# One product for each step of the merge's coefficient chain, and other gates for the pool rows' loads

## The chip, the cores and the metric

The kernel runs on one core of a Trainium2 chip. The metric is the device time of a whole execution in microseconds (us). TensorE (PE) multiplies, VectorE (DVE), ScalarE (ACT) and GpSimd (POOL) work elementwise, and SyncE (SP) issues nearly all DMA transfers. PE reads and writes nothing in DRAM: it takes operands from SBUF and leaves results in the eight banks of PSUM.

## What is computed

One encoder layer on two sequences (`x_prompt`, `x_sample`), each 1024 tokens of 1024 channels, in fp32. Cut to what matters here:

```
h = rmsnorm(x, norm_mix);  z = h @ w_in
a = pool_mixer(z[..., :512], pool_maps, pool_scale) @ w_up_pool
b = attention_branch(z[..., 512:]) @ w_up_attn
gates = sigmoid(h @ w_gate + b_gate)
x = x + (g_a * a + g_b * b) @ w_out
h = rmsnorm(x, norm_ffn)
x = x + (silu(h @ w_ffn_gate) * (h @ w_ffn_up)) @ w_ffn_down
y = rmsnorm(x, norm_final)

# end of attention_branch, three groups of four heads:
alpha  = softmax(stack(lses), axis=0)        # weights of the 3 groups
merged = sum(alpha[..., None] * outs, axis=0)
```

## The kernel before

The two sequences (s = 0, 1) follow one another. Every fp32 product is made of three single-pass matmuls: an operand is split into a rounded part (`_hi`) and the rest (`_lo`), and the small-by-small term is left out (`three`, L1207 to L1209). The projections use Strassen's scheme: a pair of weight tiles `n` takes seven **products**, numbered m = 7n + o, each of 4 x 3 = 12 matmuls of 128x512. The front of a sequence is products 0 to 132 (19 pairs); then come the up products (pool and attention rows by their up weights), `w_out`, the FFN.

The order on each engine is written out by hand: each engine has its own loop over m, and code hung on `if m == ...` stands at that place of that engine's queue. ACT makes `t_hi` (`operand_hi`, L1703) three products ahead, POOL the `t_lo` (`low_part`, L988) behind it, and PE waits for `t_ready`. After the first product of a pair ACT copies its bank out (`first_product`, `u`, L1715), and PE's third product of that pair, which adds to the same bank, waits for this copy. DVE makes the Strassen sums from PSUM (`after_product`: L2222, L2225, L2228, L2230, L2232); the last product of a pair adds to the bank that L2228 reads, and so waits for L2228.

Around m = 117 to 132 the **merge** of the three attention groups runs beside products of the pairs 16 to 18. Its **coefficient chain**: SP loads the softmax statistics (`st_all`, L697), DVE forms differences (`merge_differences`, L2325 to L2328), ACT takes the exponential (`merge_weights`, L1800), DVE normalizes (`merge_coefficients`, L2336 to L2341), ACT rounds (`round_coefficients`, L1805), DVE takes the rest (`split_coefficients`, L2348), PE turns the 24 coefficient columns (L1370) and ACT copies them out (`evict_coefficients`, L1814). Then twelve **spreads** (L1384) follow, two behind each of six products from SPREAD0 on; each writes a coefficient's row to all its channels in a bank. DVE multiplies (`merge_step`, L2368, counted by `ct_read`); POOL adds two of three groups (`merge_sum`, L1008, `two_merged`) and DVE the third (`merge_last`, L2378, `merged` after each half). There are four such pairs of sums. `MERGE0` is 118 and `SPREAD0` is 123.

The **pool rows** of the mixer (four tiles `ml` of 128x1024, 512 KB each) were written to DRAM before and are loaded (`load_mixed`, L724) into the SBUF space that the attended rows `oT` leave. ACT and DVE split them (`mix_hi` L1826, `mix_lo` L2391). The first up product needs `mix_lo` of row tile k at its matmul 3k+1, and `wu_lo`, the split up weights, which POOL makes (L1113) after `merged` and after ACT's `wu_hi` (L1835). Weights `wu_raw` are loaded at L733 and L734 (256 KB and 128 KB for each of two buffers), the gates `gl` at L743 (1 MB).

Of the kernel before, what the change touches and what calls it, by code (L numbers as in the profile page):

```python
# [84 lines left out]
VT_AFTER = {7 * (N_QK + g) + (4, 6, 7, 8)[c]: (g, c) for g in range(GROUPS) for c in range(4)}  # L85
MERGE0 = ATT0 + N_UNITS + 4


SPREAD0 = MERGE0 + 5

SUM_AFTER = {SPREAD0 + 4 + (3 * i + 1) // 2: (i // 2, i % 2) for i in range(4)}
MERGE = [(q, h, g) for q in range(2) for h in range(2) for g in range(GROUPS)]
# [167 lines left out]
def due(name, s, n):  # L260

    step = 16 if name in DMA_SEMS else 1
    return (s * PER_SEQ[name] + n) * step
# [50 lines left out]
def encoder(nc, x, w_in, maps, w_up_pool, w_up_attn, w_gate, w_out, w_fg, w_fu, w_fd,  # L314
# [3 lines left out]
    with ctx:  # L318
# [206 lines left out]
        def _(sp):  # L525
# [193 lines left out]

            def load_mixed(s, gs, batches):  # L720

                sp.wait_ge(merged, due("merged", s, batches))
                for g in gs:
                    sp.dma_start(ml[g][:, :], mix_rows[g]).then_inc(ml_in[g], 16)  # L724

# [78 lines left out]
            for s in range(SEQS):  # L804
# [6 lines left out]
                for m in range(FRONT):  # L811
# [53 lines left out]
                    if m == SPREAD0 + 3:  # L865
                        sp.wait_ge(mix_stored, due("mix_stored", s, 8))
                        load_mixed(s, range(3), 1)
                    if m == SPREAD0 + 6:
                        sp.wait_ge(ct_full, due("ct_full", s, 12))
                        load_up(s, 0)  # L870
                        load_up(s, 1)
                        load_mixed(s, range(3, 4), 2)
                    if m == FRONT - 4:
# [730 lines left out]
        def _(act):  # L1604
# [301 lines left out]
            for s in range(SEQS):  # L1906
# [34 lines left out]
                for m in range(FRONT):  # L1941
# [23 lines left out]
                    if s and m in (3, 4):  # L1965
                        final_stats(s - 1, 3 + m)
                    if m == MERGE0 - 1:
                        merge_weights(s)
                    if m == MERGE0:
                        round_coefficients(s)  # L1970
                    if m == SPREAD0 - 1:
                        evict_coefficients(s)
                    if m == SPREAD0 + 8:
                        up_hi(s, 0)
                        up_hi(s, 1)
# [100 lines left out]
        def _(dve):  # L2076
# [415 lines left out]
            for s in range(SEQS):  # L2492
# [24 lines left out]
                for m in range(FRONT + 1):  # L2517
# [23 lines left out]
                    elif stage == 1:  # L2541
                        window_sums(s, e, (2, 3))
                        window_means(s, e)
                    if m == MERGE0 - 1:
                        make_selector(s)
                        merge_differences(s)
                    if m == MERGE0:
                        merge_coefficients(s)
                        split_coefficients(s)
                    f = 2 * (m - SPREAD0 - 1)  # L2550
# [150 lines left out]
```

## Time and profile before

| | us |
|---|---|
| median of 3 runs | 2529.12 |
| lowest and highest | 2526.83, 2532.96 |
| the profiled execution: time | 2531.72 |
| its span, first to last instruction | 2529.8 |
| mean granted TensorE clock | 0.997 |

The profile is one execution. The span is what its rows cover; the time has another 1.9 us around it. A timeline row gives start, duration, engine, line, operation, output from inputs, count, and in brackets the engine's idle time ahead of it with what ended it. A matmul of 128x512 has a duration of 0.39 us but the next begins 0.23 us after it, so idle time in brackets is 0.16 us less than the delay of a start.

### The profile page before, as it was taken

Reading aid. Unit: us, or ns where it says so; the run is one execution under the profiler, and the core shown is the slowest. Engines: PE = TensorE matmul, PEld = TensorE weight load, DVE = VectorE, ACT = ScalarE, POOL = GpSimd, SP = SyncE. Lnnn points to the kernel's source line nnn. Section 1 sums busy time; section 2 is a strip of 40 time slices with the busy share of each in tenths; the row PEclk is TensorE's granted clock in tenths of the full one; section 3 lists DMA queues with packets and bytes.
Section 4 is the critical chain, followed back from the end, with each engine's and each line's share of the span. In section 5 each row is a group of like instructions: output and inputs, shape, how many; then the busy total and the mean of one; then the engine's idle time right before and its main releaser. Section 6 shows DMA issues by size and latency. Waiting matters only on the chain.

```text
span 2529.8 us, 32980 instructions
## 1 busy us (share of the span) xinstructions
PE 2495.5 (99%) x11900; PEld 2055.7 (81%) x11900; DVE 1283.3 (51%) x1784; ACT 1035.6 (41%) x2000; POOL 1712.4 (68%) x1269
## 2 busy tenths in 40 slices
PE   7999999999999999999999999999999999999998
PEld 6788878788888888888888887878888888888887
DVE  7852545653522222378988444556453222223768
ACT  5224554444533333345452345534453233233445
POOL 6666446644888888765787654574468888887544
PEclk9999999999999999999999999999999999999999
DMA  4444455472233333375453535555522333335544
GB/s 149 153 137 140 153 164 169 150 258 93 87 95 118 100 92 122 104 237 176 145 164 100 162 101 168 168 168 187 217 92 80 121 96 96 117 96 174 184 129 142
DMA packets 329024, 354.40 MB, mean 140 GB/s; under 512 B 30368, under 2 KB 236064, under 8 KB 327328
## 3 DMA queue, kind: packets, MB, share of 16 engines
q1 hardware_dynamic: 327424, 349.04, 43.7%
q10 hardware_dynamic: 1440, 3.25, 0.3%
q8 instruction: 97, 1.59, 0.3%
q14 instruction: 63, 0.52, 0.1%
HBM read 250.85 MB, written 101.38 MB: 139 GB/s over the span
## 4 chain that ended last, share of the span: by engine, by line
PE 91%; DVE 3%; ACT 1%; DMA 1%; issue 1%; POOL 1%; SPq 0%; ACTq 0%; DVEq 0%
PE ps L1207 28%; PE ps L1209 28%; PE ps L1208 28%; PE ps L1322 2%; PE ps L1283 2%; PE ps L1300 1%; DMA st_rows<-st 1%; PE ps L1340 0%; PE ps L1228 0%; ACT S L1672 0%; PE ps L1361 0%; DVE mix_lo L2391 0%; DVE X L2088 0%; PE ps L1255 0%; ACT squares L1617 0%
## 5 line engine op out<-in xcount | busy, mean ns | idle before, releaser
L1207 PE MATMUL ps<-S,t_hi 128*128 128x512 f32 (+1 forms) x2328 | 916.4, 394 | 10.7 <-ACT u L1715 4.1
L1209 PE MATMUL ps<-S,t_lo 128*128 128x512 f32 (+1 forms) x2328 | 904.4, 389 | 0.0
L1208 PE MATMUL ps<-S,t_hi 128*128 128x512 f32 (+1 forms) x2328 | 903.7, 388 | 0.0
L1207 PEld LDWEIGHTS ps<-S,t_hi 128*128 128x128 f32 x2328 | 438.7, 188 | 106.5 <-issue 12.6
L1209 PEld LDWEIGHTS ps<-S,t_lo 128*128 128x128 f32 x2328 | 438.9, 189 | 90.4
L1208 PEld LDWEIGHTS ps<-S,t_hi 128*128 128x128 f32 x2328 | 439.0, 189 | 86.2 <-issue 1.0
L988 POOL TENSOR_TENSOR t_lo<-wraw,t_hi 128x512 fp32r<-128x512 f32 x185 | 248.2, 1342 | 216.3 <-ACT t_hi L1703 213.0
L988 POOL TENSOR_TENSOR t_lo<-wraw_ff,t_hi 128x512 fp32r<-128x512 f32 x225 | 293.0, 1303 | 74.4 <-ACT t_hi L1703 70.3
L988 POOL TENSOR_TENSOR t_lo<-R,t_hi 128x512 fp32r<-128x512 f32 x154 | 221.2, 1442 | 175.4 <-ACT t_hi L1703 175.3
L1703 ACT CAST t_hi<-wraw_ff 128x512 fp32r<-128x512 f32 x225 | 139.9, 623 | 368.9 <-PE ps L1209 368.4
L1207 PE MATMUL ps<-t_hi,d_hi 128*128 128x512 f32 x616 | 240.9, 391 | 0.6 <-POOL t_lo L988 0.6
L1209 PE MATMUL ps<-t_hi,d_lo 128*128 128x512 f32 x616 | 239.9, 389 | 0.0
L1208 PE MATMUL ps<-t_lo,d_hi 128*128 128x512 f32 x616 | 239.8, 389 | 0.0
L1703 ACT CAST t_hi<-wraw 128x512 fp32r<-128x512 f32 x185 | 115.6, 626 | 244.2 <-PE ps L1209 238.0
L2443 DVE TENSOR_TENSOR d_lo<-d_raw,d_hi 128x512 fp32r<-128x512 f32 x154 | 146.4, 954 | 94.5 <-ACT d_hi L1891 93.6
L2222 DVE TENSOR_TENSOR u<-u,ps 128x512 f32<-128x512 f32 x82 | 56.2, 685 | 265.7 <-PE ps L1209 265.3
L1891 ACT CAST d_hi<-d_raw 128x512 fp32r<-128x512 f32 x154 | 95.5, 620 | 172.8 <-PE ps L1209 151.1
L2225 DVE TENSOR_TENSOR v<-u,ps 128x512 f32<-128x512 f32 x82 | 56.3, 686 | 207.4 <-PE ps L1209 207.2
L988 POOL TENSOR_TENSOR t_lo<-t,t_hi 128x512 fp32r<-128x512 f32 x74 | 97.7, 1321 | 93.6 <-ACT t_hi L1703 93.5
L988 POOL TENSOR_TENSOR t_lo<-t_ff,t_hi 128x512 fp32r<-128x512 f32 x90 | 117.6, 1307 | 31.5 <-ACT t_hi L1703 31.4
L1207 PEld LDWEIGHTS ps<-t_hi,d_hi 128*128 128x128 f32 x616 | 115.6, 188 | 25.3 <-POOL t_lo L988 1.2
L1122 POOL TENSOR_TENSOR wo_lo<-wo_raw,wo_hi 128x1024 fp32r<-128x1024 f32 x32 | 82.3, 2582 | 79.3 <-ACT wo_hi L1857 79.3
(182 smaller groups left out, 3903.3 us busy)
## 6 DMA issues: line engine op xcount, KB each, us to landing
d_raw<-d_rows SPq DMA_DIRECT2D x154, 256.0 KB, 2.8
d_rows<-act_f SPq DMA_DIRECT2D x110, 256.0 KB, 2.1
wraw_ff<-w_ffn_up SPq DMA_DIRECT2D x44, 512.0 KB, 4.6
R<-w_ffn_down SPq DMA_DIRECT2D x88, 256.0 KB, 3.1
wraw<-w_in SPq DMA_DIRECT2D x42, 512.0 KB, 5.8
sp_rows<-gst SPq DMA_DIRECT2D x80, 256.0 KB, 2.4
wraw_ff<-w_ffn_gate SPq DMA_DIRECT2D x40, 512.0 KB, 5.0
wo_raw<-w_out SPq DMA_DIRECT2D x36, 512.0 KB, 4.0
```

Source lines behind the costliest of these rows:

```text
L988: nc.gpsimd.tensor_tensor(shape(t_lo[r][:, :]), src, shape(t_hi[r][:, :]).bitcast(F32), ALU.subtract).then_inc(t_ready, 1)
L1122: nc.gpsimd.tensor_tensor(wo_lo[r][:, :], wo_raw[op % 3][:, :], wo_hi[r][:, :].bitcast(F32), ALU.subtract).then_inc(wo_ready, 1)
L1207: nc.tensor.matmul(o_ps, w[0], r[0], start=begins, stop=False, skip_group_check=True)
L1208: nc.tensor.matmul(o_ps, w[0], r[1], start=False, stop=False, skip_group_check=True)
L1209: return nc.tensor.matmul(o_ps, w[1], r[0], start=False, stop=ends, skip_group_check=True)
L1283: ins = nc.tensor.matmul(ps[:, first + h, c:c + wid], qk[p % 2][rows, 0, b * P:(b + 1) * P], qk[p % 2][rows, 1, lo:lo + wid], start=True, ...
L1322: ins = nc.tensor.matmul(ps[rows, 5, c0 + us.start * P:c0 + us.stop * P], V[p % 2][0:length, v, rows], pT[0:length, us, h * len(tiles) + c ...
L1703: nc.scalar.copy(dst, src).then_inc(thi_ready, 1)
L1891: nc.scalar.copy(d_hi[d % 4][:, :], d_raw[d % 4][:, :]).then_inc(dhi_ready, 1)
L2222: V_.tensor_tensor(u, u, b1, ALU.add).then_inc(sums_done, 1)
L2225: V_.tensor_tensor(v1[:, :], u, b2, ALU.add).then_inc(sums_done, 1)
L2443: V_.tensor_tensor(d_lo[d % 4][:, :], d_raw[d % 4][:, :], d_hi[d % 4][:, :].bitcast(F32), ALU.subtract).then_inc(d_ready, 1)
```

## The change

The chain gets later and separate places: `merge_differences` and `merge_weights` stand at m = 119 (from 117), `merge_coefficients` at 120 (from 118), `round_coefficients` and `split_coefficients` at 121 (from 118), `evict_coefficients` at 123 (from 122). PE's turn of the coefficients is behind product 122 instead of 121, and the spreads stand behind products 124 to 129 instead of 123 to 128; so do DVE's steps that read them and POOL's clearing and sums, each one product later, except POOL's fourth sum, which stays behind the low part of 132. ACT's `up_hi` stays at 131. The loads of the pool rows get gates of their own: tile 0 four steps, tile 1 POOL's second sum, tile 2 the first merged half, tile 3 ten steps (all were `merged`, one half for tiles 0 to 2 and two for tile 3). The load of the up weights moves from SP's place 129 to 130, while the first gates' load stays at 129.

```diff
-SPREAD0 = MERGE0 + 5
-SUM_AFTER = {SPREAD0 + 4 + (3 * i + 1) // 2: (i // 2, i % 2) for i in range(4)}
+WEIGHTS0 = MERGE0 + 1
+SPREAD0 = MERGE0 + 6
+SUM_AFTER = {min(SPREAD0 + 4 + (3 * i + 1) // 2, FRONT - 1): (i // 2, i % 2) for i in range(4)}
...
-            def load_mixed(s, gs, batches):
-                sp.wait_ge(merged, due("merged", s, batches))
+            def load_mixed(s, gs):
                 for g in gs:
+                    if g in (0, 3):
+                        sp.wait_ge(ct_read, due("ct_read", s, 4 if g == 0 else 10))
+                    elif g == 1:
+                        sp.wait_ge(two_merged, due("two_merged", s, 2))
+                    else:
+                        sp.wait_ge(merged, due("merged", s, 1))
                     sp.dma_start(ml[g][:, :], mix_rows[g]).then_inc(ml_in[g], 16)
...
-                    if m == MERGE0 - 1:
+                    if m == WEIGHTS0:
                         merge_weights(s)
-                    if m == MERGE0:
+                    if m == WEIGHTS0 + 2:
                         round_coefficients(s)
                     if m == SPREAD0 - 1:
                         evict_coefficients(s)
-                    if m == SPREAD0 + 8:
+                    if m == FRONT - 2:
                         up_hi(s, 0)
                         up_hi(s, 1)
...
-                    if m == MERGE0 - 1:
+                    if m == WEIGHTS0 - 2:
                         make_selector(s)
+                    if m == WEIGHTS0:
                         merge_differences(s)
-                    if m == MERGE0:
+                    if m == WEIGHTS0 + 1:
                         merge_coefficients(s)
+                    if m == WEIGHTS0 + 2:
                         split_coefficients(s)
```

On ACT, at the coefficient chain of the first sequence (`u` is the bank copy, `d` the differences), there stood:

```order
L1800 ACTIVATE d_303<-d_303 128x96 [waits diff_ready]
L1703 CAST t_hi_110<-wraw_104 128x512 [waits wraw_in1,prod_done]
L1805 CAST coef<-d_303 128x8x12 [waits coef_ready]
L1703 CAST t_hi_108<-wraw_104 128x512 [waits t_made,wraw_in1,prod_done]
L1715 COPY u_1_122<-ps 128x512 [waits sums_done,prod_done]
```

and now there stands (L1709 is `operand_hi`, L1721 the bank copy, L1806 and L1811 the chain):

```order
L1709 CAST t_hi_110<-wraw_104 128x512 [waits wraw_in1,prod_done]
L1709 CAST t_hi_108<-wraw_104 128x512 [waits t_made,wraw_in1,prod_done]
L1806 ACTIVATE d_303<-d_303 128x96 [waits diff_ready]
L1721 COPY u_1_122<-ps 128x512 [waits sums_done,prod_done]
L1709 CAST t_hi_107<-t_117 128x512 [waits t_made,wraw_in1,prod_done]
L1709 CAST t_hi_109<-wraw_104 128x512 [waits t_made,wraw_in1,prod_done]
L1811 CAST coef<-d_303 128x8x12 [waits coef_ready]
```

The wait for `coef_ready` moved from ahead of the bank copy to behind it and two more casts; the wait for `diff_ready` is still ahead of the copy.

On DVE, at the end of the merge, there stood (`mT` is the merged sum):

```order
L2368 TENSOR_TENSOR oT_169<-oT_169,ps 128x8x64 [waits ct_full]
L2225 TENSOR_TENSOR v_123<-u_0_121,ps 128x512 [waits sums_done,prod_done]
L2378 TENSOR_TENSOR mT_172<-mT_172,oT_169 128x8x64 [waits two_merged,ct_read]
L2391 TENSOR_TENSOR mix_lo_184<-ml_176,mix_hi_180 128x1024 [waits prod_done,mix_hi_ready]
L2228 TENSOR_TENSOR gst_151<-v_123,ps 128x512 [waits gst_stored1,sums_done,prod_done]
L2391 TENSOR_TENSOR mix_lo_185<-ml_177,mix_hi_181 128x1024 [waits prod_done,mix_hi_ready]
```

and now (L2374 steps, L2384 last adds, L2397 `mix_lo`, L2231 and L2234 the Strassen sums):

```order
L2231 TENSOR_TENSOR v_123<-u_0_121,ps 128x512 [waits sums_done,prod_done]
L2384 TENSOR_TENSOR mT_172<-mT_172,oT_169 128x8x64 [waits two_merged,ct_read]
L2374 TENSOR_TENSOR oT_167<-oT_167,ps 128x4x128 [waits ct_full]
L2374 TENSOR_TENSOR oT_169<-oT_169,ps 128x8x64 [waits ct_full]
L2397 TENSOR_TENSOR mix_lo_184<-ml_176,mix_hi_180 128x1024 [waits prod_done,mix_hi_ready]
L2234 TENSOR_TENSOR gst_151<-v_123,ps 128x512 [waits gst_stored1,sums_done,prod_done]
L2384 TENSOR_TENSOR mT_172<-mT_172,oT_169 128x8x64 [waits two_merged,ct_read]
L2397 TENSOR_TENSOR mix_lo_185<-ml_177,mix_hi_181 128x1024 [waits prod_done,mix_hi_ready]
```

The first `mix_lo` and the sum of the bank come ahead of the last merge add, which was ahead of both.

On SP, the loads at the end of the front now stand so:

```order
L730 DMA ml_176<-mix_rows 128x1024 [waits ct_read,mix_stored]
L730 DMA ml_177<-mix_rows 128x1024 [waits two_merged]
L730 DMA ml_178<-mix_rows 128x1024 [waits merged]
L628 DMA sp_rows<-gst_150 128x512 [waits c11_copied]
L749 DMA gl_198<-sp_rows 128x2x1024 [waits gst_stored1,gst_stored0,t_ready]
L739 DMA wu_raw_192<-up_rows 128x4x128 [waits folded_stored,ct_full]
L740 DMA wu_raw_192<-w_up_attn 128x2x128
L739 DMA wu_raw_193<-up_rows 128x4x128 [waits folded_stored]
L740 DMA wu_raw_193<-w_up_attn 128x2x128
L730 DMA ml_179<-mix_rows 128x1024 [waits ct_read]
```

Before, the load of `gl_198` stood behind that of `ml_179`, at the end of this piece; now it is ahead of the up weights.

## Rows read from the trace of the kernel before

**Rows 1.** The page's first part: busy us (share of span), instructions.
```profile
PE 2495.5 (99%) x11900; PEld 2055.7 (81%) x11900; DVE 1283.3 (51%) x1784; ACT 1035.6 (41%) x2000; POOL 1712.4 (68%) x1269
```

**Rows 2.** Waits of PE, whole span: us in total, times, longest us.
```profile
PE ps L1207 <- ACT u L1715: 4.1, 3, 2.5
...
PE ps L1207 <- DVE mix_lo L2391: 1.1, 2, 0.8
```

**Rows 3.** Windows view: stretch, us, busy and count by engine, PEclk, DMA share, GB/s.
```profile
447.40:451.80 4.40, 4.40 (x13) 3.29 (x14) 0.56 (x1) 0.88 (x2) 4.14 (x4) 0.62 0.26 87
```

**Rows 4.** Timeline of PE, first sequence, products 120, 121 and the turn.
```profile
444.48 0.39 PE L1209 MATMUL ps<-S,t_lo 128*128 128x512 f32 x1
447.38 0.47 PE L1207 MATMUL ps<-S,t_hi 128*128 128x512 f32 x1 [2.51 <-ACT u L1715]
...
451.74 1.10 PE L1370 MATMUL ps<-ident_sb,coef 128*24 128x128 f32 x8
```

**Rows 5.** Timeline of ACT, same stretch.
```profile
441.45 0.28 ACT L1800 ACTIVATE d<-d 128x96 f32<-128x96 f32 x1 [6.61 <-DVE d L2328]
...
445.96 0.27 ACT L1805 CAST coef<-d 128x96 fp32r<-128x96 f32 x1 [3.72 <-DVE d L2341]
...
446.66 0.58 ACT L1715 COPY u<-ps 128x512 f32<-128x512 f32 x1
```

**Rows 6.** Timeline of DVE, same stretch.
```profile
440.56 0.19 DVE L2325 TENSOR_TENSOR mn<-st_all 128x32 f32<-128x32 f32 x1 [4.39 <-DMA st_all<-st_rows]
...
443.69 1.33 DVE L2338 TENSOR_TENSOR wden<-d,st_all 128x32 f32<-128x32 f32 x1
...
445.67 0.26 DVE L2341 TENSOR_TENSOR d<-d,mn 128x96 f32<-128x96 f32 x1
```

**Rows 7.** Timeline of PE, second sequence, product 121.
```profile
1691.36 0.47 PE L1207 MATMUL ps<-S,t_hi 128*128 128x512 f32 x1 [0.84 <-ACT u L1715]
```

**Rows 8.** Timeline of PE, first sequence: product 129, first up product, its fourth row tile.
```profile
474.47 0.39 PE L1207 MATMUL ps<-S,t_hi 128*128 128x512 f32 x1
...
485.35 0.39 PE L1207 MATMUL ps<-mix_hi,wu_hi 128*128 128x512 f32 x1
...
487.79 0.50 PE L1207 MATMUL ps<-mix_hi,wu_hi 128*128 128x512 f32 x1 [0.24 <-DVE mix_lo L2391]
```

**Rows 9.** Timeline of PE, second sequence, the same fourth row tile.
```profile
1730.77 0.50 PE L1207 MATMUL ps<-mix_hi,wu_hi 128*128 128x512 f32 x1 [0.83 <-DVE mix_lo L2391]
```

**Rows 10.** Timeline of POOL, first sequence: second and fourth merge sum.
```profile
467.49 1.56 POOL L1008 TENSOR_TENSOR mT<-mT,oT 128x512 f32<-128x512 f32 x1
...
477.44 1.56 POOL L1008 TENSOR_TENSOR mT<-mT,oT 128x512 f32<-128x512 f32 x1
```

**Rows 11.** Timeline of DVE, first sequence, end of the front.
```profile
474.26 2.19 DVE L2378 TENSOR_TENSOR mT<-mT,oT 128x512 f32<-128x512 f32 x1
...
477.47 0.69 DVE L2225 TENSOR_TENSOR v<-u,ps 128x512 f32<-128x512 f32 x1
479.10 1.17 DVE L2378 TENSOR_TENSOR mT<-mT,oT 128x512 f32<-128x512 f32 x1 [0.94 <-POOL mT L1008]
480.16 1.23 DVE L2391 TENSOR_TENSOR mix_lo<-ml,mix_hi 128x1024 fp32r<-128x1024 f32 x1
481.29 0.70 DVE L2228 TENSOR_TENSOR gst<-v,ps 128x512 f32<-128x512 f32 x1
481.89 1.89 DVE L2391 TENSOR_TENSOR mix_lo<-ml,mix_hi 128x1024 fp32r<-128x1024 f32 x1
...
484.30 3.44 DVE L2391 TENSOR_TENSOR mix_lo<-ml,mix_hi 128x1024 fp32r<-128x1024 f32 x2
```

**Rows 12.** Timeline of SP's queue, same stretch: issues.
```profile
471.46 1.27 SPq L724 DMA_DIRECT2D ml<-mix_rows  x3
...
476.09 0.57 SPq L733 DMA_DIRECT2D wu_raw<-up_rows  x1
```

**Rows 13.** Timeline of ACT, same stretch: the up weights have landed.
```profile
480.63 0.93 ACT L1835 CAST wu_hi<-wu_raw 128x512 fp32r<-128x512 f32 x2 [2.36 <-DMA wu_raw<-w_up_attn]
```

More of the change, by code:

```diff
@@ L866, in _ @@
                         sp.wait_ge(mix_stored, due("mix_stored", s, 8))
-                        load_mixed(s, range(3), 1)
+                        load_mixed(s, range(3))
                     if m == SPREAD0 + 6:
@@ L871, in _ @@
                         load_up(s, 1)
-                        load_mixed(s, range(3, 4), 2)
+                        load_mixed(s, range(3, 4))
                     if m == FRONT - 4:
```

## The prediction

> **What bounds the kernel now.** I read the page's busy shares first: PE is busy 99% of the span, the next engine 68% [rows 1]. So the time is PE's, and an edit on the other engines is worth what it takes from, or adds to, PE's waits. The list of PE's waits names two that touch the merge: 4.1 us for ACT's bank copy `u`, of which one wait is 2.5, and 1.1 us for DVE's `mix_lo` [rows 2]. The timeline shows both in place. I number the merge's products as the kernel does.
>
> At **product 121** PE should have started 0.23 us behind the row at 444.48, at 444.71, and started at 447.38: 2.67 us late [rows 4]. It waited for the copy at 446.66. ACT had been free to copy since product 119 ended near 442, but stood in `round_coefficients` until 445.96, 3.72 us idle, because DVE's normalizing ended only with the row at 445.67 [rows 5, 6]. That chain began when `st_all` landed at 440.56, after 4.39 us of DVE waiting, and one of its small operations took 1.33 us where its likes take 0.19 [rows 6]. In the second sequence the same wait is 0.84 us, a late start of 1.00 [rows 7].
>
> Then comes a second cost in the first sequence: the granted clock is 0.62 on average from 447.4 to 451.8 [rows 3], so most of product 121 ran at 1.2 GHz after PE's idle 2.51 us. It took 451.74 - 447.38 = 4.36 us [rows 4]. At 2.4 GHz a product takes (485.35 - 474.47) / 4 = 2.72 us [rows 8]; 1.64 us were lost.
>
> At the **front's end** PE starts the up products at 485.35 without waiting, and would reach the fourth row tile nine matmuls (2.04 us) later, at 487.39; it starts that at 487.79, 0.40 late [rows 8]. In the second sequence it is 0.83 idle, 0.99 late [rows 9]. Both wait for the last `mix_lo`.
>
> **Part 1: the chain behind the bank copy.** ACT's wait for `coef_ready` is now behind the copy and two casts. `merge_weights` is still ahead of it, but its input was ready at 441.45 [rows 5], while the copy may start near 442 and is needed at 444.71 with its 0.58: 2 us of room. The coefficients, ready at 445.94, are needed by PE's turn behind product 122, at 444.71 + 2 x 2.72 = 450.15: 4 us of room, with ACT's and DVE's two 0.3 us steps in it. The bank copy's wait should go whole. Gain: 2.67 + 1.64 in the first sequence and 1.00 in the second, **5.3 us**. Of PE's own work nothing is added or removed; the eight turns and twelve spreads only change places. What is late next there is `t_lo` of product 122, whose cast no longer waits for the coefficients either; I cost it at nothing, hidden behind product 121.
>
> The Trainium skill (TensorE: Matmul & The Clock Gate, Part 1) says that where a change of the clock falls differs between runs of the same kernel. No row here shows a second execution. If the drop is missing in the timed runs before, the gain is 1.6 us less; the terms above hold without this.
>
> **Part 2: everything behind the chain comes one product later, the front's end does not.** This is the cost. Take POOL's second sum as the origin. It follows the low part of a product whose cast waits for PE, so it moves with the products. Before, it starts at 467.49, 17.86 us ahead of the front's end at 485.35 [rows 8, 10]. Now one product less lies between: 17.86 - 2.72 = 15.14. Times after its start:
>
> - before, the last two steps end where L2225 starts, at 477.47, 9.98 after the origin [rows 11]. Now L2225 (0.6) stands ahead of the third merge add: 10.6.
> - `mix_lo` 0 fills the wait for POOL's fourth sum (0.94 in the row at 479.10 [rows 11]). Alone it takes 1.13 of the queue (480.16 to 481.29), with POOL busy 1.8 (481.89 to 483.70, from its 1.89), and the fourth sum (1.56 [rows 10]) runs just then: it ends at 11.7 to 12.4.
> - L2228, 0.6: 12.3 to 13.0. PE's product 132 adds to the bank it reads and would start at 15.14 - 2.72 = 12.42: a new wait of 0 to 0.6 us, where 481.29 + 0.70 was 0.6 us ahead of 485.35 - 2.72 = 482.63.
> - the last merge add, 1.06 (479.10 to 480.16): 13.4 to 14.1.
> - then `mix_lo` 1, a sum, `mix_lo` 2 and 3. Before this took 484.30 + 3.44 - 481.89 = 5.85 with POOL's `wu_lo` beside it; free of POOL it would be 3 x 1.13 + 0.6 = 4.0. The end is at 17.4 to 19.9.
>
> PE needs the last one at 15.14 + 2.04 = 17.18. So PE is **0.2 to 2.7 us** late in the first sequence, where it was 0.40. I take 2.2, near the upper end, because POOL's `wu_lo` now starts with the last merge add and covers all three.
>
> Here the row and a rule part a little. Rows 11 show the same add at 1.17 and 2.19, and `mix_lo` at 1.23 and 1.89, by what POOL does. The Trainium skill (SBUF — State Buffer, two separate sides) says that a DVE operation with two SBUF inputs and a reading GpSimd operation hold a shared port in turn, each for its whole instruction. By it `mix_lo` 0 could wait for the whole fourth sum, 1.56 us instead of the 0.7 in my upper end, and the sum would be up to 0.9 us worse in each sequence. It speaks against this placing; it alone would put the time some 1.8 us above mine, inside my range.
>
> **Part 3: the loads.** The three first pool tiles no longer come together at 471.46 [rows 12] but spread from four steps on, so their bytes are out of the way sooner: a gain where they bind. Against it the first gates' load (1 MB) is now ahead of the up weights, which were issued at 476.09. Counting bytes from the first half's `merged` (471.46, 3.97 after the origin) to the first up weights' landing: before 3 x 512 + 256 + 384 KB, now 512 + 256 + 1024 + 384 KB, the same 2176 KB. Before they took 480.63 - 471.46 = 9.17 us [rows 12, 13]; now `wu_hi` can start at 13.1, the second one at about 14.4, and ACT's queue goes on: `up_hi` to 15.3, `mix_hi` 2 to 16.3, `mix_hi` 3 to 17.3 if tile 3 has landed (its 512 KB more, at the same rate 2.2 us, by 16.7), and `mix_lo` 3 to 18.5 or 19.1. That is 1.3 to 1.9 us late for PE, no later than DVE's own chain gives. POOL's `wu_lo` for the first up product, from `merged` at about 13.8, takes about 2 and is ready near the front's end, 0.2 to 0.7 us late, inside the same delay. If in the second sequence the loads are slower by the 0.6 us that its wait was longer than the first's [rows 8, 9], it is 2.8 us late there. I bound each sequence by 0.2 and 4.0.
>
> The loads of the chain's start change too: L2230 now is not behind the differences, so SP stores its result and issues the next gate weights (1 MB) some 4 us sooner, right behind `st_all`. The room of 2 us on ACT covers a later landing; cost nothing, at most the old wait again.
>
> **The sum.** Gain 5.3; loss at the front's end 2.2 + 2.8 - 0.40 - 0.99 = 3.6; net **-1.7 us**. Against the profiled execution's own 2531.72 that is 2530.0. That execution lies 2.6 us above the median of the three runs, which spread over 6.1; taken from the median, 2529.12 - 1.7 = **2527.4**.
>
> **The rivals.** *The front's end hides the shift*: DVE's chain ends at its lower bound in both sequences. For it: 4.0 us is what the rows without POOL make, and the first `mix_lo` falls in an old wait. Against it: POOL's `wu_lo` can't be elsewhere. Delay 0.2 + 0.2 against 1.4: a gain of 5.3 + 1.0 = 6.3, or 5.3 if it stays as it was. Time 2522.8 to 2523.8.
> *The new wait brings the clock down*: the last pool tile or the weights land later than reckoned, PE idles 4.5 us at the start of the up products in each sequence, and the clock falls as it did after 2.51 us at product 121, 1.64 more each. 2 x (4.5 + 1.64) - 1.4 - 5.3 = +5.6: 2534.7, **slower**. For it: the gates' megabyte is put ahead. Against it: the waits there are in three or four pieces with matmuls between. It decides from (5.1 + 6.7) / 2 = 5.9 us of loss in each sequence.
> *The wait at 121 only changes its name*: `st_all` lands over 2 us later behind the heavier traffic, ACT stands in `merge_weights`, and the copy is late as before. Gain 0 to 2, loss 3.6 and no drop of the clock saved: 2529 to 2533, most likely 2531. Against it: `st_all` is issued ahead of those loads.
>
> **How the numbers follow.** A measurement of this kernel can tell about 0.2% (5.1 us) from no change. Forecast 0.62, hidden shift 0.18, clock at the up products 0.07, changed name 0.13. The hidden shift gives faster only with its full size: with a part of the forecast's spread, faster 0.2; slower is the clock's rival and a little of the last, 0.09; the same 0.71. The low end takes the hidden shift in, 2523.0; the high end takes 4.0 us of delay in both sequences and one drop of the clock, 8.0 - 1.4 - 5.3 + 1.6 = +2.9: 2532.0.
>
> **What would show it.** Right: no wait of PE for `u` at L1721 over 0.3 us near product 121, granted clock 1.0 there, the front's end about 4.3 us sooner in the first sequence; then PE waiting for `mix_lo` (L2397), `wu_lo` or L2234 for 2 to 3 us together in each sequence. Wrong: `u` still named; waits at the front's end no longer than before, or over 4 us, or with the clock at half behind them.

## The result, and the profile after

| | before, us | after, us |
|---|---|---|
| median (20 runs each) | 2528.05 | 2533.68 |
| lowest and highest | 2526.30, 2534.09 | 2530.38, 2536.11 |
| the profiled execution: time | 2531.72 | 2532.82 |
| its span | 2529.8 | 2530.9 |

The ratio after to before is 1.0020, 95% interval 1.0014 to 1.0027: the changed kernel is 3.5 to 6.8 us slower. I had forecast 2527.4 in a range up to 2532.0. The profiled executions differ by 1.1 us only, the medians by 5.6: the first profile of before was not a typical one, as two further executions show below. The measured median lies outside the range.

The page's first part and the list of PE's waits of the changed kernel, to be set beside [rows 1] and [rows 2]:

```profile
PE 2493.7 (99%) x11900; PEld 2052.6 (81%) x11900; DVE 1285.5 (51%) x1784; ACT 1035.7 (41%) x2000; POOL 1706.1 (67%) x1269
...
PE ps L1213 <- DVE mix_lo L2397: 4.1, 4, 1.4
...
PE ps L1213 <- ACT u L1721: 1.7, 2, 0.9
...
PE ps L1213 <- POOL wu_lo L1119: 0.8, 2, 0.5
```

The work is the same. The waits for `u` fell from 4.1 to 1.7 (0.77 of them at the span's start, in no relation to the merge; before had such a wait too), those for `mix_lo` rose from 1.1 to 4.1, and 0.8 for `wu_lo` is new. The timeline of PE shows where: product 121 and the start of the up products, in the first sequence and then in the second.

```profile
444.54 0.47 PE L1213 MATMUL ps<-S,t_hi 128*128 128x512 f32 x1 [0.91 <-ACT u L1721]
...
481.80 0.50 PE L1213 MATMUL ps<-mix_hi,wu_hi 128*128 128x512 f32 x1 [0.49 <-POOL wu_lo L1119]
...
484.82 0.50 PE L1213 MATMUL ps<-mix_hi,wu_hi 128*128 128x512 f32 x1 [1.36 <-DVE mix_lo L2397]
...
486.50 0.51 PE L1213 MATMUL ps<-mix_hi,wu_hi 128*128 128x512 f32 x1 [0.71 <-DVE mix_lo L2397]
...
1726.97 0.50 PE L1213 MATMUL ps<-mix_hi,wu_hi 128*128 128x512 f32 x1 [0.33 <-POOL wu_lo L1119]
...
1731.67 0.50 PE L1213 MATMUL ps<-mix_hi,wu_hi 128*128 128x512 f32 x1 [0.70 <-DVE mix_lo L2397]
```

From the first up product to its fourth row tile PE needs 2.04 us without waits. It took 487.79 - 485.35 = 2.44 before [rows 8]; now it takes 486.50 - 481.80 = 4.70, and 1731.67 - 1726.97 = 4.70 again. I call this stretch **the up start** below; it is the ruler of this study.

The waits at the up products go back to one thing. SP's queue, ACT, DVE and POOL of the changed kernel, first sequence:

```profile
471.23 0.37 SPq L749 DMA_DIRECT2D gl<-sp_rows  x1
472.97 0.58 SPq L739 DMA_DIRECT2D wu_raw<-up_rows  x1
```
```profile
479.70 0.93 ACT L1841 CAST wu_hi<-wu_raw 128x512 fp32r<-128x512 f32 x2 [6.40 <-DMA wu_raw<-w_up_attn]
480.90 0.93 ACT L1841 CAST wu_hi<-wu_raw 128x512 fp32r<-128x512 f32 x2 [0.27 <-DMA wu_raw<-w_up_attn]
481.74 1.99 ACT L1832 CAST mix_hi<-ml 128x1024 fp32r<-128x1024 f32 x2
```
```profile
475.37 2.22 DVE L2397 TENSOR_TENSOR mix_lo<-ml,mix_hi 128x1024 fp32r<-128x1024 f32 x1
...
479.22 1.20 DVE L2397 TENSOR_TENSOR mix_lo<-ml,mix_hi 128x1024 fp32r<-128x1024 f32 x1
...
482.82 3.62 DVE L2397 TENSOR_TENSOR mix_lo<-ml,mix_hi 128x1024 fp32r<-128x1024 f32 x2 [1.79 <-ACT mix_hi L1832]
```
```profile
474.96 1.55 POOL L1014 TENSOR_TENSOR mT<-mT,oT 128x512 f32<-128x512 f32 x1 [1.68 <-DVE oT L2374]
480.47 4.89 POOL L1119 TENSOR_TENSOR wu_lo<-wu_raw,wu_hi 128x512 fp32r<-128x512 f32 x4 [3.96 <-ACT wu_hi L1841]
```

The up weights are issued behind the gates' megabyte and are there 479.70 - 472.97 = 6.7 us later, after ACT has stood 6.40 us. Before it was 480.63 - 476.09 = 4.5 [rows 12, 13]. ACT's queue has the casts of the last two pool tiles behind them, DVE's last two `mix_lo` wait for these (1.79), and since POOL's `wu_lo` waited for the same landing, it runs beside them: 3.62 us for two that take 1.20 each alone. PE starts the up products 481.80 - 479.70 = 2.10 behind the landing, and the fourth row tile 6.80 behind it. In the second sequence ACT's cast started at 1724.82, and the distances are 2.15 and 6.85. So the up start hangs on that landing, and its 4.70 us is the length of a fixed sequence of engine work behind it.

### The profile page after: what moved, and what is told of

It is laid out like the page before. It is cut to its first block and busy times, and to the rows that moved or that the text cites. A ratio compares the mean times of both kernels' runs of the same rounds, so it can differ in the third digit from the quotient of the medians.

```text
span 2530.9 us, 32980 instructions
## 1 busy us (share of the span) xinstructions
PE 2493.7 (99%) x11900; PEld 2052.6 (81%) x11900; DVE 1285.5 (51%) x1784; ACT 1035.7 (41%) x2000; POOL 1706.1 (67%) x1269
## 5 line engine op out<-in xcount | busy, mean ns | idle before, releaser
L1709 ACT CAST t_hi<-wraw_ff 128x512 fp32r<-128x512 f32 x225 | 139.9, 623 | 369.6 <-PE ps L1215 368.4
L1709 ACT CAST t_hi<-wraw 128x512 fp32r<-128x512 f32 x185 | 115.7, 626 | 247.5 <-PE ps L1215 243.8
L2231 DVE TENSOR_TENSOR v<-u,ps 128x512 f32<-128x512 f32 x82 | 56.3, 687 | 198.6 <-PE ps L1215 198.2
```

The costliest lines, as they stand in the source:

```text
L1709: nc.scalar.copy(dst, src).then_inc(thi_ready, 1)
L2231: V_.tensor_tensor(v1[:, :], u, b2, ALU.add).then_inc(sums_done, 1)
```

## Experiments

Times are medians; ratios are to the kernel before, run on the same chip beside it (its medians were 2527.51, 2526.97 and 2527.07 in the three batches). I set two theories against each other, named as in the expectations. Theory G: the gates' load ahead of the up weights makes the loss. Theory S: the spreads and DVE's chain, one product later, make it.

### Two more executions of before, one of after

No edit.

> The kernel before, unchanged, for a second profile. Its first profiled execution took 2531.72 us, its median over 32 runs is 2527.5. Theory V (that execution was not a usual one): here PE's wait for u at product 121 of the first sequence is near the 1.1 us that the kernel with only other load gates shows, not 2.5; the clock stays full there; from product 117 to the fourth row tile of the up products it takes about 50.5 us, not 54.1. Rival: the wait of 2.5 us and the drop of the clock are there again, and the missing 4 us lie elsewhere.

> The changed kernel, unchanged, for a second profile. If its waits are a matter of its order and not of the execution, the pieces of the first profile come again: PE waits 2.3 to 2.6 us at the start of the up products in each sequence, from product 117 to the fourth row tile 54.0 and 52.7 us within 0.7, and from the second norm of the second sequence to the end 628.8 us as in the undisturbed ones, or 629.7 as in its first profile.

> The kernel before once more, for the spread of its wait for u at product 121: the first profiled execution had 2.51 us and a fall of the granted clock behind it, another 0.47. If the long wait is usual, 1.5 to 2.5 us; if it was one execution's, under 1 us and no fall of the clock.

The kernel before took 2525.59 and 2526.39 us, the changed one 2531.98. In the first of the two further executions of before PE's timeline shows, at product 121 of each sequence and at the second sequence's up start:

```profile
444.31 0.47 PE L1207 MATMUL ps<-S,t_hi 128*128 128x512 f32 x1 [0.47 <-ACT u L1715]
...
1685.88 0.47 PE L1207 MATMUL ps<-S,t_hi 128*128 128x512 f32 x1 [0.54 <-ACT u L1715]
...
1725.26 0.50 PE L1207 MATMUL ps<-mix_hi,wu_hi 128*128 128x512 f32 x1 [0.78 <-DVE mix_lo L2391]
```

DVE says why: the statistics landed sooner against the products, 6.0 us ahead of the due start of product 121 (443.68), where in the first profile it was 4.15.

```profile
437.66 0.19 DVE L2325 TENSOR_TENSOR mn<-st_all 128x32 f32<-128x32 f32 x1 [2.51 <-DMA st_all<-st_rows]
```

The wait for `u` is 0.47, not 2.51, and nothing behind it runs at a lower clock; the other one has 0.37 and 0.51. (That DVE's wait here is 2.51 too is chance.) Over all six executions of the study in which the chain stood at its old places, twelve waits, it was 0.24 to 1.13, and once 2.51: 9.5 us in twelve, 0.8 each. The 2.51 us and the fall of the granted clock to 0.62 [rows 3, 4] belonged to one of the three profiled executions of before. Five of its 20 timed runs lie over 2530 us too; whether for the same reason, no profile shows.

The second execution of the changed kernel has the same 4.70 us at both up starts as its first profile. From the start of product 117 to the fourth row tile, the stretch that the expectations count, it took 53.70 and 53.11 us in the two sequences, against 54.03 and 52.67 in the first profile; before took 50.33 and 51.07, then 50.24 and 50.68, and in its first profile 54.09 and 51.41.

### The gates' load alone put back

On the changed kernel:

```diff
                     if m == SPREAD0 + 6:
                         sp.wait_ge(ct_full, due("ct_full", s, 12))
                         load_up(s, 0)
                         load_up(s, 1)
                         load_mixed(s, range(3, 4))
-                    if m == FRONT - 4:
                         sp.wait_ge(t_ready, due("t_ready", s, FRONT - 7))
                         load_gates(s, 0)
```

> The changed kernel with one edit: the first gates' load (1 MB) goes back behind the last pool tile's load. In the changed kernel PE loses 0.49 + 1.36 + 0.71 us at the start of the up products in the first sequence and 0.33 + 1.37 + 0.70 in the second. Theory G (the gates' megabyte ahead of the up weights is what makes them late): the up weights land about 2.5 us sooner after their issue (4.5 us instead of 6.7), the waits there fall to 1 us or less in each sequence, and the time falls by 3 to 4 us against the changed kernel (2533.7), to about 2530. Theory S (DVE's own chain, one product later, is what binds): the last mix_lo is bound by DVE with POOL beside it, the waits stay over 2 us in each sequence, and the time falls by less than 1.5 us.

2527.55 (11 runs), ratio 1.0001 (0.9992 to 1.0009): all of the loss is gone with this one load, 6 us where I expected 3 to 4. ACT, DVE and PE of this kernel:

```profile
475.96 0.93 ACT L1840 CAST wu_hi<-wu_raw 128x512 fp32r<-128x512 f32 x2 [3.30 <-DMA wu_raw<-w_up_attn]
...
481.42 1.05 ACT L1831 CAST mix_hi<-ml 128x1024 fp32r<-128x1024 f32 x1 [1.41 <-DMA ml<-mix_rows]
```
```profile
480.29 1.71 DVE L2396 TENSOR_TENSOR mix_lo<-ml,mix_hi 128x1024 fp32r<-128x1024 f32 x1
482.50 1.23 DVE L2396 TENSOR_TENSOR mix_lo<-ml,mix_hi 128x1024 fp32r<-128x1024 f32 x1 [0.50 <-ACT mix_hi L1831]
```
```profile
480.97 0.50 PE L1212 MATMUL ps<-mix_hi,wu_hi 128*128 128x512 f32 x1 [0.29 <-POOL wu_lo L1118]
...
483.78 0.50 PE L1212 MATMUL ps<-mix_hi,wu_hi 128*128 128x512 f32 x1 [0.45 <-DVE mix_lo L2396]
```

The up weights, issued at 472.32, were there in 3.6 us instead of 6.7. The up starts took 2.81 and 2.77 instead of 4.70. What is left over 2.04, 0.8 us in each sequence, and the 0.3 us ahead of it for `wu_lo` are the most that theory S can claim here; before had 0.6 on average. Even there the last wait is for ACT and the last pool tile's landing (1.41), not for DVE's own queue. By this count that small loss and the small gain at product 121 about cancel.

### The gates' load alone put ahead, on the kernel before

```diff
                     if m == SPREAD0 + 6:
+                        sp.wait_ge(t_ready, due("t_ready", s, FRONT - 7))
+                        load_gates(s, 0)
                         sp.wait_ge(ct_full, due("ct_full", s, 12))
                         load_up(s, 0)
                         load_up(s, 1)
                         load_mixed(s, range(3, 4), 2)
-                    if m == FRONT - 4:
-                        sp.wait_ge(t_ready, due("t_ready", s, FRONT - 7))
-                        load_gates(s, 0)
```

> The kernel before with one edit: the first gates' load (1 MB) goes ahead of the up weights at SP's place 129, as the change has it; nothing else of the change. Theory G: the up weights and the last pool tile land 2 to 3 us later, PE loses 1.5 to 2.5 us more at the start of the up products in each sequence, and the time is 3 to 5 us above the kernel before, some 2531 to 2532. Rival (the order of these loads costs only where the merge is late too): the one product more of room that the old spreads leave covers it, and the time stays within 1 us of 2527.5.

2536.11 (5 runs), ratio 1.0038 (1.0024 to 1.0051): worse than the whole change, and twice the loss that I expected. ACT and PE in the first sequence:

```profile
480.63 0.92 ACT L1834 CAST wu_hi<-wu_raw 128x512 fp32r<-128x512 f32 x2 [7.04 <-DMA wu_raw<-w_up_attn]
```
```profile
482.71 0.50 PE L1206 MATMUL ps<-mix_hi,wu_hi 128*128 128x512 f32 x1 [1.78 <-POOL wu_lo L1112]
```

The up weights took 8.6 us (472.01 to 480.63), PE waited 1.78 and 1.57 us for `wu_lo` ahead of the up products, and the up starts took 4.69 and 4.70. Here spreads, sums and `mix_lo` stand where they always stood, so theory S has no part in it. In the first sequence the granted clock fell too, before the fourth row tile. The windows view (stretch, us, busy and count of PE, PEld, DVE, ACT, POOL, PEclk, DMA share, GB/s):

```profile
484.00:486.00 2.00, 0.68 (x3) 0.26 (x2) 2.00 (x2) 1.98 (x3) 2.00 (x2) 0.55 0.96 343
486.00:488.00 2.00, 1.98 (x4) 1.07 (x5) 2.00 (x3) 1.99 (x2) 0.27 (x1) 0.50 0.38 118
488.00:490.00 2.00, 2.00 (x6) 1.61 (x5) 2.00 (x2) 1.27 (x2) 0.00 (x0) 0.50 0.35 131
490.00:492.00 2.00, 2.00 (x8) 1.54 (x8) 0.81 (x2) 0.00 (x0) 0.00 (x0) 0.74 0.25 72
```

From the fourth row tile to one and the same transposition of the second norm (L1254) took 163.82 us there (487.40 to 651.22), against 162.11 in the second sequence (1734.44 to 1896.55): 1.7 us for the lower clock.

### Half of the gates' load put back

On the changed kernel:

```diff
-            def load_gates(s, j):
+            def load_gates(s, j, part=0):
...
+                if j == 0:
+                    sp.dma_start(gl[0][:, part, :], sp_rows[4 + part]).then_inc(gl_in[0], 16)
+                    return
...
                         load_mixed(s, range(3, 4))
+                        load_gates(s, 0, 1)
```

Part 0 stays ahead of the up weights, part 1 goes behind the last pool tile (the semaphore counts, changed to match, are left out here).

> The changed kernel with its first gates' load cut in two: 512 KB of it still ahead of the up weights, the other 512 KB behind the last pool tile. Theory (bytes ahead of the up weights delay them, ACT's mix_hi and the last mix_lo): with 1 MB ahead the up weights took 6.7 us from issue to ACT's wu_hi, with none 3.6; so with half about 5.1, the start of the up products up to the fourth row tile 3.5 to 4.0 us (4.70 with all, 2.8 with none), and a time about half way between 2533.7 and 2527.5: 2530 to 2531. Rival (it is DVE's and POOL's chain, not the bytes): 4.7 us stays there, 2533. Rival (a threshold: half of it is hidden): 2.8 us and 2527.5.

2528.22 (11 runs), ratio 1.0006 (0.9997 to 1.0015): with 512 KB ahead the median is 1.1 us over the kernel before, which the interval doesn't tell from nothing, where with 1 MB it was 5.6. In the first sequence the up weights took 4.5 us (471.36 to 475.81) and the up start 2.76, as with none ahead. In the second it took 4.01:

```profile
1727.21 0.50 PE L1217 MATMUL ps<-mix_hi,wu_hi 128*128 128x512 f32 x1 [1.68 <-DVE mix_lo L2401]
```
```profile
1723.83 1.05 ACT L1836 CAST mix_hi<-ml 128x1024 fp32r<-128x1024 f32 x1 [0.99 <-DMA ml<-mix_rows]
```
```profile
1722.87 1.36 DVE L2401 TENSOR_TENSOR mix_lo<-ml,mix_hi 128x1024 fp32r<-128x1024 f32 x1 [0.28 <-ACT mix_hi L1836]
1724.91 2.24 DVE L2401 TENSOR_TENSOR mix_lo<-ml,mix_hi 128x1024 fp32r<-128x1024 f32 x1 [0.69 <-ACT mix_hi L1836]
```

So the cost is not in proportion to the bytes, nor is it the landing of the up weights that did it here: in the second sequence these took only 4.1 us (1714.54 to 1718.61). The last pool tile was there 0.63 us behind PE's start of the up products (1723.20), against 0.20 in the first sequence, and the last `mix_lo`, beside POOL's `wu_lo`, took 2.24 us against 1.42. My "half way" missed by 2 us; the rival with a threshold holds in one sequence and half in the other.

### The chain alone, and the changed kernel with the chain at its old places

On the kernel before, the chain's new places only (turn and spreads as before):

```diff
-                    if m == MERGE0 - 1:
+                    if m == MERGE0 + 1:
                         merge_weights(s)
-                    if m == MERGE0:
+                    if m == MERGE0 + 3:
                         round_coefficients(s)
```

and DVE's three steps at `MERGE0 + 1`, `+ 2`, `+ 3`.

> The kernel before with one edit: the coefficient chain at its new places (119, 120, 121), while the turn of the coefficients, the spreads, the sums and all loads stay where they were. Theory S: the cost of the change is the later spreads alone, so this one keeps the gain at the bank copy and has the old waits at the up products (0.2 to 0.8 us): 1 to 3 us below the kernel before (2528.05), 2525 to 2527. Rival: the turn behind product 121 now waits for the split coefficients, 1 to 2 us in each sequence, and the bank copy's gain is given back there: 2527 to 2529.

2526.52 (11 runs), ratio 0.9996 (0.9987 to 1.0005): 1.0 us less, which the interval doesn't resolve. PE no longer waits for `u` at 121 and waits 0.23 and 0.20 for `coef` at the turn instead:

```profile
447.94 1.04 PE L1370 MATMUL ps<-ident_sb,coef 128*24 128x128 f32 x8 [0.23 <-DVE coef L2348]
```

The opposite, the changed kernel with these five steps back at 117 and 118:

> The changed kernel with the coefficient chain back at its old places (117 and 118) on DVE and ACT; the spreads, sums and loads stay one product later. Theory A (the chain's new places gain what the bank copy's wait was worth and the later spreads cost more): PE waits for u again by 0.8 to 2.5 us in each sequence, the waits at the start of the up products stay at 2.3 to 2.6 us, and the time is 1 to 3 us above the changed kernel, 2535 to 2537. Rival B (the new places gain nothing, since something else holds the copy): the time is that of the changed kernel within 1 us.

2534.15 (10 runs), ratio 1.0026 (1.0017 to 1.0036). The waits for `u` are 0.67 and 0.79:

```profile
444.29 0.47 PE L1213 MATMUL ps<-S,t_hi 128*128 128x512 f32 x1 [0.67 <-ACT u L1721]
```

The up starts are 4.69 and 4.71. The median is 0.5 us over the changed kernel's and the ratio 0.0006 over its ratio; the intervals overlap, so what the chain's places are worth isn't told by this pair. (By the time, the expectation's rival B holds; the waits lie just under the range of its theory A.) Everything else of the change is still there, and so is all of the loss.

### The pool rows' gates alone

On the kernel before, only `load_mixed` with its four gates.

> The kernel before with one edit: each pool tile's load has its own gate (four steps, the second sum, the first merged half, ten steps). Nothing else moves, so the gates' load stays behind. Theory: the first three tiles' bytes are gone when the up weights are issued, these land 1 to 2 us sooner, and the wait for the last mix_lo in the second sequence falls from 0.83 us to the first one's 0.2: the time is that of the kernel before or up to 1 us below. Rival: DVE binds there anyway and nothing changes.

2526.23 (11 runs), ratio 0.9995 (0.9986 to 1.0004). The up starts are 2.29 and 2.27, where the three executions of before had 2.62 on average, and no wait for `mix_lo` is left. By that view this part wins about 0.7 us; the median is 1.3 lower, which the interval doesn't tell from nothing.

### The exponential behind the bank copy

On the changed kernel, ACT:

```diff
-                    if m == WEIGHTS0:
+                    if m == WEIGHTS0 + 1:
                         merge_weights(s)
```

> The changed kernel with the exponential of the coefficient chain on ACT one more place later, behind the bank copy u of pair 17, so that no step of the chain stands ahead of that copy. Theory: the rest of the wait for u in the first sequence (0.5 to 0.9 us in two executions) goes, under 0.1; the waits at the up products stay (4.70 us to the fourth row tile in both sequences). Time about 0.5 us under the changed kernel's, which one look can't tell. Rival (the copy was late for its own Strassen sum, or for the bank): the wait for u stays at 0.5 to 0.9.

One execution. The rest of the wait for `u` is gone. ACT of the changed kernel, and then of this one:

```profile
443.64 0.28 ACT L1806 ACTIVATE d<-d 128x96 f32<-128x96 f32 x1 [4.79 <-DVE d L2334]
443.82 0.57 ACT L1721 COPY u<-ps 128x512 f32<-128x512 f32 x1
```
```profile
440.76 0.59 ACT L1721 COPY u<-ps 128x512 f32<-128x512 f32 x1 [2.10 <-PE ps L1215]
...
443.47 0.28 ACT L1806 ACTIVATE d<-d 128x96 f32<-128x96 f32 x1 [1.60 <-DVE d L2334]
```

The copy moved from 443.82 to 440.76. The up starts stayed 4.70 and 4.70, and this time the clock fell behind both of them:

```profile
486.00:488.00 2.00, 2.00 (x7) 1.51 (x6) 2.00 (x2) 1.02 (x1) 0.00 (x0) 0.50 0.47 171
...
1732.00:1734.00 2.00, 2.00 (x6) 1.61 (x5) 2.00 (x3) 0.85 (x1) 0.00 (x0) 0.50 0.52 184
```

Both stretches behind them are 1.6 us longer (163.70 and 163.69 for 162.1), and the execution took 2534.18. The same stretch of the changed kernel's own profile is at full clock, after waits of 0.49, 1.36 and 0.71 us where this one had 0.69, 1.38 and 0.71:

```profile
486.00:488.00 2.00, 1.50 (x7) 1.24 (x8) 2.00 (x3) 2.00 (x2) 0.00 (x0) 1.00 0.95 331
```

The length of the waits doesn't decide it: the second execution of the changed kernel stayed at full clock behind 0.74, 1.38 and 0.71.

### The parts that gain, together

The kernel before with the chain's places and the pool rows' gates, spreads and gates' load as before; and the same with the exponential behind the copy:

```diff
-                    if m == MERGE0 + 1:
+                    if m == MERGE0 + 2:
                         merge_weights(s)
```

> The kernel before with the chain at its new places and the new gates of the pool tiles' loads, but the old spreads and the gates' load behind. Alone the two gave 2526.5 and 2526.2 against 2527.5. If they act at different places (bank copy at 121; up weights' landing at the front's end) they add up: 0.4 to 1 us below either, about 2525.5. Rival: both only shift the same wait, and the time is 2526.2 again.

> The kernel before with the chain at its new places, its exponential behind the bank copy too, and the pool rows' new gates; the spreads and the gates' load where they were before. If each of the three is worth what it showed alone (chain about 1.0, pool rows' gates 1.3, no wait for u 0.2 to 0.5): 2.3 to 2.8 us under the kernel before, 2524.5 to 2526; PE waits under 0.3 us in all at products 118 to 132 and nothing at the up products. If the gains overlap: 1 to 1.5 us under it, as the combination without the exponential's move gave (2525.97 against 2526.97).

The first gave 2525.97 (11 runs), ratio 0.9997 (0.9988 to 1.0006), with up starts of 2.30 and 2.31. The second gave 2527.04 (11 runs), ratio 0.9999 (0.9990 to 1.0008), no gain, where I had expected 1 to 2.8 us. It has no wait for `u`, and up starts of 2.24 and 2.29; but in the first sequence PE waits for the coefficients:

```profile
449.16 1.04 PE L1375 MATMUL ps<-ident_sb,coef 128*24 128x128 f32 x8 [1.10 <-DVE coef L2353]
```
```profile
446.22 1.21 DVE L2343 TENSOR_TENSOR wden<-d,st_all 128x32 f32<-128x32 f32 x1
```

With the turn still behind product 121, the chain has no room for one small operation of 1.21 us (its likes take 0.19; the last section shows what held it). Neither is shown to beat the kernel before.

## Why the prediction was wrong, point by point

Two steps failed. The gain of Part 1 was read from one execution that was not typical: 5.3 us were counted and 1.5 are there, a fall of the clock included. Part 3 counted bytes, found the total unchanged, and so let the gates' load ahead of the up weights cost nothing beyond DVE's own chain: that load made the loss, 5.1 us of waits for the 3.6 that I had put down to DVE's chain, and 1.0 for the clock. That 3.6 and 5.1 are not far apart is luck: with the gates' load behind, DVE's chain is still one product later and the loss is gone.

**Part 1, the gain of 5.3 us: mechanism right, size wrong.** The steps "2.67 + 1.64 in the first sequence" took one execution for the kernel. In twelve sequences with the old places the wait was 0.8 us on average; in the eight of the changed kernel's two executions, the one with the gates' load back and the one with half of it, it was 0.91, 0.53, 0.22 and five times nothing over 0.2. The gain is some 0.6 us a sequence, 1.2 in all, and 0.3 for the fall of the clock, once in those twelve; the chain alone gave 1.0, not told from nothing. I knew that the profiled execution lay 2.6 us above the median and yet took its gain off the median in full. The sentence on the Trainium skill (TensorE: Matmul & The Clock Gate, Part 1) names something that the traces show, though not at this place. The fall of the clock at 121 was in one of three executions of before, but that one had by far the longest wait too; at the up starts, behind waits as long, the clock fell in three cases of ten. The sentence let me take only 1.6 of the 4.3 us for uncertain; the wait itself was as untypical.

**"2 us of room" for `merge_weights`: wrong.** The input was ready at 441.45 [rows 5], 3.3 us ahead of the due start of product 121; after the change it was ready at 443.64, 0.2 behind it, since on DVE a Strassen sum (L2238) now stands ahead of the differences:

```profile
442.15 0.69 DVE L2238 TENSOR_TENSOR gst<-u,ps 128x512 f32<-128x512 f32 x1 [5.96 <-DMA sp_rows<-gst]
442.76 0.18 DVE L2331 TENSOR_TENSOR mn<-st_all 128x32 f32<-128x32 f32 x1
```

The statistics, issued at 435.97, were not waited for; DVE stood 5.96 us ahead of the sum. The view names its store. In the last combination, with the same order, it names PE at 442.64, so I leave open which of the two let the sum go. Either way a wait of 0.91 stayed in the first sequence: the rival of the changed name, at 0.13, was partly right in its outcome, and wrong in its cause, a late landing of the statistics.

**"4 us of room" for the coefficients: right as the change has it**, with the turn behind 122, and wrong for a turn behind 121, where 0.2 to 1.1 us are waited.

**Part 2, DVE's chain: there, but smaller.** With the gates' load out of the way PE is 0.45 us late at the first up product and 0.8 more at the fourth row tile, 1.2 against the 2.2 and 2.8 that I took. POOL's second sum did not quite move with the products: from it to the front's end (due at 480.93 + 0.23 = 481.16, without the wait for `wu_lo`) there were 15.7 us, not 15.14, which helped by 0.6. The first `mix_lo` took 2.22 us (475.37) where one alone takes 1.20; POOL's sum ran until 476.51, 1.14 us into it. So it lost 1.0, nearly the whole overlap, and not the 0.7 of my upper term. The Trainium skill (SBUF — State Buffer, SBUF: two separate sides) has the one wait for the other's whole instruction; this row agrees with it better than with my estimate. It cost little, because the place had slack. Product 132's new wait was 0.1 us.

**Part 3, the loads: the step that failed at the front's end.** "The same 2176 KB ... now `wu_hi` can start at 13.1": with POOL's second sum at 465.43 as the origin it started at 14.3. Counted bytes told neither how the 1 MB, issued 1.7 us ahead, would share the engines with the weights nor what stood idle for it: from issue to landing 6.7 us, not 4.5. The Trainium skill (DMA: Bandwidth & Descriptors, Queues, rings and completion order) says that each DMA engine consumes a queue's descriptors in ring order. The experiments agree: in the first sequence 3.6, 4.5 and 6.7 us with none, half and all of the megabyte ahead on the changed kernel, and 4.5 and 8.6 with none and all of it on the kernel before. They would agree as well with engines that share themselves out between both loads; no run here separates the two. Then "ACT ... `mix_lo` 3 to 18.5 or 19.1 ... no later than DVE's own chain": it ended at 486.44 - 465.43 = 21.0. 1.2 us of that is the landing, the rest POOL's `wu_lo`, which I had set beside DVE's chain but not beside these two: 3.62 us for 2.4. PE was 3.3 us late at the fourth row tile (486.50 against 481.16 + 2.04), and 3.15 in the second sequence.

**The sum again, as measured.** Waits for `u`: -1.2, and -0.3 for the fall of the clock there. Up starts: 2 x 2.66, less the three executions of before, which had 0.40 + 0.99, 0.28 + 0.94 and 0.30 + 0.59, mean 1.2: +4.1. Waits for `wu_lo` ahead of them: 0.49 + 0.33 and 0.54 + 0.74 in two executions, +1.0. Clock: ten up starts of 4.7 us were profiled (five executions of four kernels), and in or behind three of them it fell to half, 1.6 to 1.7 us each; at the eighteen shorter ones it never fell. If that is the rate, 0.3 x 2 x 1.65 = +1.0. Together +4.6, where 5.6 was measured with an interval of 3.5 to 6.8. The clock's share is an estimate and rests on three events. What is left is inside the interval.

The way from -1.7 to +5.6, 7.3 us, is then 3.8 for the gain that was not there, 1.5 for the larger loss at the front's end, 1.0 for the clock, and 1.0 that is not accounted for.

One view goes without this sum. From product 117 to the fourth row tile the changed kernel took 106.7 and 106.8 us in both sequences together, at full clock; the two further executions of before took 101.4 and 100.9, its first profile 105.5. Against the two it is 5.6 us more in this stretch alone, as much as the medians differ.

**The rivals.** "The new wait brings the clock down", at 0.07, came nearest in time (2534.7), but by luck. PE idled 2.6 us in each sequence, not 4.5, and the clock fell in 3 of 10 up starts, not in all: some 5 us less loss than the rival has. It still took my gain of 5.3 off, 3.8 too much. The two errors nearly cancel. I had set against it that the waits come in pieces with matmuls between; the clock fell now and then all the same, as in the rows at 484 to 490. The sign of the forecast failed through Part 1: with a gain of 1.5 instead of 5.3 even my own loss of 3.6 gives +2.1, slower though under what can be told.

## What to carry to other kernels

Before a wait is priced, look whether the execution is a typical one: if it lies above the median, its longest single wait may be the reason, and the gain is then to be taken from several executions. When a large load that nothing needs yet is moved ahead of a small one that a whole stage hangs on, cost the small one's time from issue to landing, then everything that stands behind it on each engine; a total of bytes that stays the same says nothing. Check for a moved step what now stands ahead of it on its own engine, as well as what it no longer holds up.

## What was not expected of the hardware

The length of the up start was 4.69 to 4.71 us in ten of ten sequences with the megabyte ahead, in five executions of four kernels whose up weights landed at different times: once one landing binds, what follows repeats to 0.02 us. Against that, the granted clock in or after such a start was 0.5 in three of ten and 1.0 in seven, and waits as long stood on both sides.

The small DVE operations of the coefficient chain take 0.19 us as a rule (0.26 for 128x96). But in the fourteen profiled executions 44 of them took 0.92 to 1.34 us, two to four in each execution. What held them shows in POOL's timeline, first of the last combination (beside the row at 446.22), then of the kernel before (beside the 1.33 us in [rows 6]):

```profile
446.09 1.29 POOL L993 TENSOR_TENSOR t_lo<-wraw,t_hi 128x512 fp32r<-128x512 f32 x1 [0.95 <-ACT t_hi L1708]
```
```profile
443.69 1.29 POOL L1045 TENSOR_TENSOR wraw<-wraw,t 128x512 f32<-128x512 f32 x1
```

DVE's operation ended at 447.43 and POOL's at 447.38; in the other pair it was 445.02 and 444.98. All 44 ended 0.05 to 0.12 us behind such an operation of POOL, also one with two inputs in SBUF. So a short dependent chain on DVE must be costed with what POOL does beside it, 0.7 to 1.1 us for each encounter here. No run was made that moves POOL's operations away.
